# Latent attention of a two-layer trunk: row sums by a column of ones, scaling after the value product, scores two units ahead, fewer projection products

## The reference

```python
def mla_project(p, q_norm_w, w_uq, kv_norm_w):
    c_q, c_kv, k_pe = split_cols(p, (256, 128, 32))
    q = (rms_norm(c_q, q_norm_w) @ w_uq).reshape(B, L, 8, 64 + 32)
    return q[..., :64], q[..., 64:], rms_norm(c_kv, kv_norm_w), k_pe
...
kv = (ckv @ w_ukv).reshape(B, L, 8, 64 + 64)      # keys without position, values
q_pe, k_pe = apply_axial_rope(q_pe), apply_axial_rope(k_pe)   # latent tokens alone
...
s = (einsum('bqhd,bkhd->bhqk', qn, k_nope) + einsum('bqhr,bkr->bhqk', qp, k_pe)) * MLA_SCALE
pr = softmax(s, axis=-1)
o = einsum('bhqk,bkhd->bqhd', pr, v)
```

## Time and profile before

| | us |
|---|---|
| median of 3 runs | 4058.32 (4054.43 to 4075.35) |
| profiled execution, time | 4057.85 |
| profiled execution, span | 4056.2 |
| PE busy in the span | 3291.5 (81%) |
| DVE busy | 1720.3 (42%) |
| ACT busy | 1016.4 (25%) |
| mean granted TensorE clock | 0.829 of full speed |

### The profile page before, as it was taken

How to read it: one execution, slowest core, us unless ns; L and a number is a source line. 1 busy time by engine, 2 the same in 40 slices (tenths; PEclk the granted TensorE clock), 3 DMA queues, 4 the chain that set the end, 5 groups by cost and what they waited for, 6 DMA issues and landing times.

```text
span 4056.2 us, 44516 instructions
## 1 busy us (share of the span) xinstructions
PE 3291.5 (81%) x18879; PEld 2612.8 (64%) x18879; DVE 1720.3 (42%) x2442; ACT 1016.4 (25%) x1361; POOL 41.8 (1%) x44
## 2 busy tenths in 40 slices
PE   8798776568778769999969877656767775999996
PEld 3698433356556669997769843335656664888884
DVE  0226333443343442220042633245353444888886
ACT  1311122210100031110031012211010033777774
POOL 0000000000000000000000000000000000000001
PEclk9896676688787789999989667667687686999997
DMA  7220000011111032221102000000000005999995
GB/s 298 93 74 22 3 0 0 0 52 63 42 52 42 35 121 73 72 73 63 63 32 73 22 3 0 0 0 1 1 1 1 2 1 233 385 397 398 395 393 218
DMA packets 63073, 384.97 MB, mean 95 GB/s; under 512 B 6640, under 2 KB 12720, under 8 KB 21808
## 3 DMA queue, kind: packets, MB, share of 16 engines
q1 hardware_dynamic: 53296, 343.95, 22.1%
q0 software_dynamic: 5328, 19.40, 1.3%
q10 hardware_dynamic: 4272, 19.06, 1.2%
HBM read 356.01 MB, written 26.38 MB: 94 GB/s over the span
## 4 chain that ended last, share of the span: by engine, by line
PE 79%; DVE 12%; ACT 4%; DVEq 2%; issue 2%; DMA 1%; POOL 0%; ACTq 0%; SPq 0%; POOLq 0%
PE ps L436 12%; PE ps L1016 9%; PE ps L440 6%; PE ps L942 5%; PE ps L1020 5%; PE ps L459 4%; PE ps L686 3%; PE ps L588 3%; PE ps L799 3%; PE ps L703 3%; PE ps L812 3%; PE ps L811 2%; PE ps L715 2%; DVE st L1673 1%; PE ps L496 1%
## 5 line engine op out<-in xcount | busy, mean ns | idle before, releaser
L436 PE MATMUL ps<-work_r,work_r 128*128 128x320 f32 x3328 | 521.4, 315 | 84.7 <-DVE work_r L1479 84.7
L1084 ACT ACTIVATE work<-ps 128x512 f32<-128x512 f32 (+9 forms) x489 | 198.9, 439 | 1534.9 <-PE ps L829 328.0
L436 PEld LDWEIGHTS ps<-work_r,work_r 128*128 128x128 f32 x3328 | 502.7, 192 | 86.6 <-ACT work_r L1084 44.2
L1016 PE MATMUL ps<-hi_r,sw_r 128*128 128x512 f32 x1632 | 397.5, 397 | 17.9 <-ACT hi_r L1084 11.0
L1016 PEld LDWEIGHTS ps<-hi_r,sw_r 128*128 128x128 f32 x1632 | 309.2, 191 | 82.5 <-issue 18.6
L440 PE MATMUL ps<-work_r,work_r 128*128 128x320 f32 x1664 | 260.9, 309 | 0.0
L1980 DVE TENSOR_TENSOR raw_r<-ring,hi_r 128x2048 fp32r<-128x2048 f32 x104 | 233.6, 2288 | 38.1 <-ACT hi_r L1084 37.9
L440 PEld LDWEIGHTS ps<-work_r,work_r 128*128 128x128 f32 x1664 | 248.3, 188 | 0.0
L1980 DVE TENSOR_TENSOR raw_r<-work,hi_r 128x2048 fp32r<-128x2048 f32 x100 | 224.7, 2288 | 35.5 <-ACT hi_r L1084 35.5
L1084 ACT ACTIVATE hi_r<-ring 128x2048 fp32r<-128x2048 f32 x104 | 193.5, 1909 | 68.2 <-PE ps L1020 57.3
L1084 ACT ACTIVATE hi_r<-work 128x2048 fp32r<-128x2048 f32 x100 | 186.2, 1910 | 68.3 <-PE ps L1020 66.7
(11 more groups left out here) (320 smaller groups left out, 4537.7 us busy)
## 6 DMA issues: line engine op xcount, KB each, us to landing
ring<-stream_d SPq DMA_DIRECT2D x217, 1024.0 KB, 5.5
work<-stream_d SPq DMA_DIRECT2D x100, 1024.0 KB, 8.3
moe_x<-work POOLq DMA_DIRECT2D x17, 512.0 KB, 4.8
work<-moe_x SPq DMA_DIRECT2D x17, 512.0 KB, 10.2
moe_y<-work ACTq DMA_DIRECT2D x17, 512.0 KB, 8.1
sw<-sw_d ACTq DMA_DIRECT2D x2, 2336.0 KB, 18.8
x<-x_in ACTq DMA_DIRECT2D x1, 2560.0 KB, 22.1
y<-x SPq DMA_DIRECT2D x5, 512.0 KB, 3.5
```

What stands on the lines that cost most here:

```text
L436: mm(out, stat(hi, k), mov(x_, k, i), start=(k == 0 and x_ == 0), stop=False)
L1016: mm(ps[:, bank, :], a[:, k * P:(k + 1) * P], moving(w_, k), start=(k == 0 and a is hi), stop=False)
L1084: return act(dst, src, ACT.Copy)
```

## The change

Three edits in `mla`, on PE, ACT and DVE alike, with the same sizes and the same slots of SBUF but for small ones.

- **Norms.** The sums are taken by token: squares as weights, two columns of ones as the moving side (30 passes), so a block of 20 columns holds all of them. Root and reciprocal run on 20 columns. The score scale goes into the query's factor with its sign turned. `spread`, a helper that was there, brings the factors back onto all rows (24 passes of 64 or 128 columns, written out to PSUM), and the three multiplications read them there.
- **Projections.** The rotary partners of four heads are made by one product of 128 features (4 products a layer where there were 16). The keys of two heads are made by one product of 128 features, between the heads' queries.
- **The loop.** Units run block by block, the 8 context units first. The scale of the row and its sum are gone from DVE and ACT: the row sum comes from a 65th column of ones beside each head's values. The value product runs once a unit with the turned block as weights and 65 moving columns (queries on the rows), and DVE divides the 64 outputs by the 65th on the way out. `features` turns the outputs of 8 heads back once a block. Scores stand two units ahead on PE, maxima two ahead on DVE.

```diff
...
-                for hf in range(2):
-                    cols = slice(hf * HALF, (hf + 1) * HALF)
-                    mm(ps[:, 4 + hf, 0:HALF], ones, slot(38)[:, cols], start=True, stop=False)
-                    mm(ps[:, 4 + hf, 0:HALF], ones, slot(39)[:, cols], start=False, stop=True)
-                    last = mm(ps[:, 6 + hf, 0:HALF], ones, slot(23)[:, cols], start=True, stop=True)
+                for c in range(NT):
+                    cols = slice(c * P, (c + 1) * P)
+                    mm(ps[:, 4, 4 * c:4 * c + 2], slot(38)[:, cols], ones[:, 0:2], start=True, stop=False)
+                    mm(ps[:, 4, 4 * c:4 * c + 2], slot(39)[:, cols], ones[:, 0:2], start=False, stop=True)
+                    last = mm(ps[:, 4, 4 * c + 2:4 * c + 4], slot(ML_TMP)[:, cols], ones[:, 0:2], start=True, stop=True)
                 last.then_inc(S("ml_ss"), 1)
+                pe.wait_ge(S("ml_rc"), at("ml_rc", l, 1))
+                spread(slice(0, P), 4, 0, 4)
+                spread(slice(0, P), 6, 2, 4).then_inc(S("ml_bc"), 1)
                 pe.wait_ge(S("ml_c"), at("ml_c", l, 1))
+                for g in range(2):
+                    for k in range(2):
+                        a = W_UQR + (k * MH + 4 * g) * ROPE
+                        last = mm(ps[:, 4 + g, 0:LAT], sw[:, a:a + P], slot(PJ_CQ + k)[:, SEQ:T], start=(k == 0), stop=(k == 1))
+                    last.then_inc(S("ml_p"), 1)
...
-                        wr = sw[:, W_UQR + (k * MH + h) * ROPE:W_UQR + (k * MH + h + 1) * ROPE]
-                        mm(ps[0:QK, 2 * u + 1, 0:SEQ], w, cq[:, 0:SEQ], start=(k == 0), stop=(k == 1))
-                        last = mm(ps[64:96, 4 + u, 0:LAT], wr, cq[:, SEQ:T], start=(k == 0), stop=(k == 1))
+                        last = mm(ps[0:QK, 2 * u + 1, 0:SEQ], w, cq[:, 0:SEQ], start=(k == 0), stop=(k == 1))
+                    if h % 2:
+                        i = h // 2
+                        if i:
+                            pe.wait_ge(S("ml_kf"), at("ml_kf", l, i))
+                        w = sw[:, W_UK + i * P:W_UK + (i + 1) * P]
+                        mm(ps[:, 6, 0:LAT], w, slot(PJ_CKV)[:, SEQ:T], start=True, stop=True)
+                        last = mm(ps[:, 7, SEQ:SEQ + PAST], w, sw[:, W_CKV:W_CKV + PAST], start=True, stop=True)
+                        last.then_inc(S("ml_k"), 1)
...
-                    b = 2 * (n % 2)
+                    j, h = divmod(n, MH)
+                    out = ml_scores(n)
...
                 def values(n):
-                    h, j = divmod(n, NT)
-                    e = h % 2
-                    if j not in (0, NT - 1):
-                        return
+                    j, h = divmod(n, MH)
+                    if n:
+                        pe.wait_ge(S("ml_of"), at("ml_of", l, n))
                     pe.wait_ge(S("ml_pt"), at("ml_pt", l, n + 1))
-                    if h:
-                        pe.wait_ge(S("ml_of"), at("ml_of", l, 2 * h - 1 if j == 0 else 2 * h))
-                    if j == 0:
-                        last = mm(ps[64 * e:64 * e + 64, 7, 0:P], vt[:, 0, h * VD:(h + 1) * VD], ptc,
-                                  start=True, stop=True)
-                    else:
-                        for k in range(5):
-                            last = mm(ps[64 * e:64 * e + 64, 6, 0:LAT], vt[:, 1 + k, h * VD:(h + 1) * VD],
-                                      pt[:, k, :], start=(k == 0), stop=(k == 4))
+                    chunks = range(1) if j == 0 else range(1, 6)
+                    for i, c in enumerate(chunks):
+                        last = mm(ml_out, slot(ML_PT + n % 2)[:, i * P:(i + 1) * P], ml_v[:, c, h, :],
+                                  start=(i == 0), stop=(i == len(chunks) - 1))
                     last.then_inc(S("ml_o"), 1)
 
+                def features(j):
+                    pe.wait_ge(S("ml_of"), at("ml_of", l, MH * (j + 1)))
+                    if j:
+                        pe.wait_ge(S("ml_ff"), at("ml_ff", l, j))
+                    for g in range(4):
+                        last = pe.transpose(ml_feat[:, g], ml_o[:, j, g * P:(g + 1) * P], ident)
+                    last.then_inc(S("ml_ft"), 1)
+
                 scores(0)
+                scores(1)
                 for n in range(MH * NT):
-                    if n + 1 < MH * NT:
-                        scores(n + 1)
-                    pe.wait_ge(S("ml_n"), at("ml_n", l, n + 1))
+                    pe.wait_ge(S("ml_e"), at("ml_e", l, n + 1))
+                    if n + 2 < MH * NT:
+                        scores(n + 2)
                     if n:
                         pe.wait_ge(S("ml_pt"), at("ml_pt", l, n))
-                    for k in range(1 if n % NT == 0 else 5):
-                        last = pe.transpose(ps[:, 4 + k // 4, (k % 4) * P:(k % 4 + 1) * P],
-                                            slot(21 + n % 2)[:, k * P:(k + 1) * P], ident)
+                    for k in range(1 if n < MH else 5):
+                        last = pe.transpose(ml_turned[:, k // 4, (k % 4) * P:(k % 4 + 1) * P],
+                                            slot(ML_P + n % 2)[:, k * P:(k + 1) * P], ident)
                     last.then_inc(S("ml_t"), 1)
                     if n:
                         values(n - 1)
+                    if n >= MH and n % MH == 3:
+                        features(n // MH - 1)
                 values(MH * NT - 1)
+                features(NT - 1)
...
-                act(slot(38, 2), slot(38, 2), ACT.Sqrt).then_inc(S("ml_rt"), 1)
+                act(factor, factor, ACT.Sqrt).then_inc(S("ml_rt"), 1)
...
                 def exponent(n):
                     sc.wait_ge(S("ml_m"), at("ml_m", l, n + 1))
                     if n >= 2:
                         sc.wait_ge(S("ml_t"), at("ml_t", l, n - 1))
-                    b, s = 2 * (n % 2), 4 * (n % 2)
-                    if n % NT == 0:
-                    act(o, i, ACT.Exp, bias=st8[:, s + 1:s + 2], scale=MLA_SCALE,
-                        accum_out=st8[:, s + 2:s + 3]).then_inc(S("ml_e"), 1)
+                    out = slot(ML_P + n % 2)
+                    o, i = (out[:, 0:P], ml_scores(n)[:, 0, 0:P]) if n < MH else (halves(out), ml_scores(n))
+                    act(o, i, ACT.Exp, bias=st8[:, n % 4:n % 4 + 1], scale=-1.0).then_inc(S("ml_e"), 1)
...
+                def features(j):
+                    sc.wait_ge(S("ml_ft"), at("ml_ft", l, j + 1))
+                    copy(tiles(2, 4)[:, :, j * P:(j + 1) * P], ml_feat).then_inc(S("ml_ff"), 1)
...
                     if n + 1 < MH * NT:
                         exponent(n + 1)
                     sc.wait_ge(S("ml_t"), at("ml_t", l, n + 1))
-                    if h and j < 2:
-                        sc.wait_ge(S("ml_o"), at("ml_o", l, 2 * h - 1 + j))
+                    if n >= 2:
+                        sc.wait_ge(S("ml_o"), at("ml_o", l, n - 1))
+                    out = slot(ML_PT + n % 2)
...
+                        copy(out[:, 0:512], ml_turned[:, 0])
+                        copy(out[:, 512:640], ml_turned[:, 1, 0:P]).then_inc(S("ml_pt"), 1)
+                    if n >= MH and n % MH == 4:
+                        features(n // MH - 1)
+                features(NT - 1)
...
-                ve.wait_ge(S("ml_ss"), at("ml_ss", l, 1))
-                ts(halves(slot(38)), ps[:, 4:6, 0:HALF], 1.0 / 256, EPS, ALU.mult, ALU.add)
-                ts(halves(slot(39)), ps[:, 6:8, 0:HALF], 1.0 / 128, EPS, ALU.mult, ALU.add).then_inc(S("ml_ms"), 1)
-                ve.wait_ge(S("ml_rt"), at("ml_rt", l, 1))
-                v.reciprocal(slot(38, 2), slot(38, 2))
...
+                ve.wait_ge(S("ml_ss"), at("ml_ss", l, 1))
+                ts(fs[:, :, 0], sums[:, :, 0], 1.0 / 256, EPS, ALU.mult, ALU.add)
+                ts(fs[:, :, 1], sums[:, :, 1], 1.0 / 128, EPS, ALU.mult, ALU.add).then_inc(S("ml_ms"), 1)
...
+                v.reciprocal(factor, factor)
+                ve.drain()
+                ts(fs[:, :, 0], fs[:, :, 0], -MLA_SCALE, None, ALU.mult).then_inc(S("ml_rc"), 1)
+                ve.wait_ge(S("ml_bc"), at("ml_bc", l, 1))
+                for k in range(2):
+                    stt(halves(slot(PJ_CQ + k)), halves(slot(PJ_CQ + k)), V(l, V_QN + k), ps[:, 4:6, 0:HALF], ALU.mult, ALU.mult)
+                stt(halves(slot(PJ_CKV)), halves(slot(PJ_CKV)), V(l, V_KVN), ps[:, 6:8, 0:HALF], ALU.mult, ALU.mult).then_inc(S("ml_c"), 1)
...
+                v.memset(ml_v[:, :, :, VD:VD + 1], 1.0)
...
                 def maxima(n):
                     ve.wait_ge(S("ml_s"), at("ml_s", l, n + 1))
-                    b, s = 2 * (n % 2), 4 * (n % 2)
-                    if n % NT == 0:
-                        v.tensor_reduce(st8[:, s:s + 1], ps[:, b, 0:P], AX.X, ALU.max)
+                    low = st8[:, n % 4:n % 4 + 1]
+                    if n < MH:
+                        last = v.tensor_reduce(low, ml_scores(n)[:, 0, 0:P], AX.X, ALU.min)
                     else:
```

(23 more changed lines are left out.)

126 lines of the change are left out of this document (54 added, 72 removed).

## The result

The changed kernel takes 3769.84 us (median of four runs; 3764.5 to 3776.4) against 4063.4 (four runs, the three known before the prediction and one more): a ratio of 0.927, 95% interval 0.924 to 0.929. The profiled execution went from 4057.85 to 3764.5 us, 293 less, where the prediction had 266 less.

What follows compares the result with a forecast made beforehand. The prediction took the loop to be bound by a chain through PE, DVE and ACT, with no engine full. Loop -109, projections -21 and norms -3 make -133 us a layer, -266 for both: 3792 us, 8-in-10 range 3745 to 3870.

Steps and rivals of the forecast that it cites:

- The chain: Old loop: PE and DVE take turns, scores behind transposes and transposes behind DVE, 5.31 us a latent unit.
- every wait is covered: New loop: other PE work covers the waits for exponential, copies and output bank, so PE runs without a pause.
- The price of a unit: New loop: a latent unit takes PE 2.73 us of passes at full clock, 2.85 with changes of group.
- the 0.12 for changes of group: New loop: about 0.12 us a latent unit for three changes of group on PE.
- the second rival: Value passes: weights don't hide behind 65 columns, perhaps 0.16 us a pass, not 0.11; 3830 us, chance 0.12.
- The clock: New loop: granted clock 1.0, after a start at 0.50 lasting about three latent units.
- the term for three slow units: Start of the new loop: three latent units at clock 0.50 add 3 x 2.55 = 8 us a layer.
- The rival of a loop at 0.50: New loop: the clock stays at 0.50 for much or all of it; 3946 us, chance 0.10.
- Transposes: New loop: transposes count as PE activity for the full clock, against the Trainium skill; a fifth of the unit's work.
- Projections and norms: Before the loop: projections 36 us against 57, -21 a layer; norms -3 a layer, between -6 and 0.
- the two unknown prices: Norms: 30 summing passes at 0.22 make 6.6 us; 24 spreading passes 2.6 to 5.3 us, taken as 5.
- The sum: Whole kernel: -133 us a layer, -266 for both, from 4057.85 to 3792 us.

Runs made afterwards that it cites:

- first two experiments: Kernel before with scores two units ahead on PE: 3844.85 us; kernel before, one unit ahead, without reciprocal and scaling of the row block: 3877.37 us.
- the kernel of 130 columns: Changed kernel with 130 moving columns in each value pass, the neighbour head's half thrown away: 3785.31 us.
- the woven kernel: Changed kernel with the context units put one by one between latent ones: 3771.27 us, ratio 0.930.

## Why the prediction was right

**The chain.** That PE and DVE take turns, with scaling and scores at the links, held: taking either link away makes most of the pauses go (first two experiments). The prediction didn't say which of the two carries the gain, and the answer is that it isn't divisible. Its reading that every wait is covered held as well, with 2.4 us of pauses in 106. One link of its chain is misread, without effect on the sum: the exponential isn't in it. The transposes of the earlier trace rows start at 558.86, while the exponential that began at 558.14 still runs; they wait for the scaling, so the chain is maximum, negative, scaling, transposes, scores.

**The price of a unit.** 2.85 was put, 2.74 measured, and 2.73 was its sum of passes: the 0.12 for changes of group isn't there. From start to start five transposes take 0.54 us, ten value passes 1.07 and four score passes 1.13. The pass of 65 columns, put at 0.11 from 40-column passes, is 0.107; the second rival, weights not hidden (0.16 a pass, chance 0.12), fell with that and again with the kernel of 130 columns.

**The clock.** Put: 1.0 with three latent units at 0.50. Measured: 13 us at 0.50, of which the context units' end is a part. The step that was mis-sized is this one with its neighbours: 105.7 less 32 x 2.74 leaves 18 us for start, context, turns and end, where the prediction had 26 (117 less 91). Together with the unit's 3.5 us that is the 11 us a layer by which the loop came out better. About half of the 8 us is the term for three slow units, 3 x 2.55 = 8. What latent units did at 0.50 was this:

```profile
524.04 2.44 PE L696 MATMUL ps<-work 96*128 96x320 f32 x4
...
526.82 2.44 PE L696 MATMUL ps<-work 96*128 96x320 f32 x4
...
529.59 2.44 PE L696 MATMUL ps<-work 96*128 96x320 f32 x4
...
531.82 1.27 PE L728 MATMUL ps<-const,work 128*128 128x128 f32 x5
```

Three groups of scores and one of transposes, and no value product: against 1.29 and 0.71 us at full clock that is 3 x 1.15 + 0.56 = 4.0 us. The rest of the difference, in start, context, turns and end, wasn't taken apart. The rival of a loop at 0.50 (0.10) held for 13 of the 106 us; from 540 us on the full units run at 1.00.

**Transposes.** The prediction went by the 20 transposes of the earlier trace rows, and the kernel with four times as many agrees with them (1.00 from 540 us on).

**Projections and norms.** -22.4 for -21, and -2.6 for -3. In the norms the two unknown prices came out as taken, 30 sums in 6.5 us for 6.6 (465.74 to 472.28) and 24 spreading passes in 5.3 for 5. The granted clock was 0.50 and 0.53 in these two stretches, and the spreading passes cost 0.22 us each, the upper end of their range:

```profile
473.93 5.33 PE L518 MATMUL ps<-const,wend 128*128 128x128 f32 x24 [1.65 <-DVE wend L1672]
```

**The sum.** 3792 against 3764.5 profiled: 23 of the 27 us are the loops, 2 the projections less the norms, and 2 to 3 lie outside the changed parts.

## What to carry to other kernels

Where two engines take turns, find every way of breaking the chain before choosing: a reordering of a few lines gave 109 of 120 us here, and the rest of the new loop 12 more. A pause of the matrix engine is paid twice if its clock falls with it, so a stretch in which PE idles can be worth more than its idle time (here 67 us of pauses and 52 of busy time). Once PE is full, count passes, not arithmetic: a float32 pass with 128-column weights cost 0.107 us for 65 moving columns and 0.112 for 130.

## What the runs showed of the hardware that was not expected

- Value passes of 65 and of 130 columns take 0.107 and 0.112 us, but in the loop's first part, short units, the granted clock was 0.50 for 13 us with the first (in both layers) and 1.00 with the second (one run, both layers): the loop was 4.6 us shorter, with columns that are thrown away.
- The loop bound by pauses gave 222.8 to 232.1 us with one and the same code, the loop bound by PE 105.68 in both layers.
- In the stretch between the loops 14 us of 1670 come and go between profiles of the same code (at a clock of 0.86 and 0.85 in the changed and the woven kernel), more than what both loops together gained in three of the experiments.
